# Attention output made feature by token: values as weights in two column strips, inverse sums widened by small products

## The reference, cut to what matters

```python
# per layer; concat over three groups of heads: A (recurrence, 256 columns), B and C (attention, 384 each)
o_a, s_a = hgrn_mixer(...)                       # (T, 256)
o_g = blocked_attention(q, k, v)                 # B: 6 query heads, 2 key/value heads, head width 64
o_w = banded_attention(q, k, v, k_ctx, v_ctx, sink)   # C: |t-s| <= 128, plus a sink logit in the sum
#   p = softmax(scores);  o = einsum('bkgqs,bskd->bqkgd', p, v)
x = x + g1 * (jnp.concatenate([o_a, o_g, o_w], axis=-1) @ w_out)
```

## Time and profile before

| | |
|---|---|
| median of 3 runs | 1646.12 us (1644.6 to 1650.44) |
| the profiled execution | 1649.72 us, span of the core 1647.9 us |
| TensorE matmul, busy | 1400.3 us, 85% |
| TensorE weight load, busy | 881.6 us, 53% |
| VectorE, busy | 566.8 us, 34% |
| ScalarE, busy | 358.0 us, 22% |
| GpSimd, busy | 210.7 us, 13% |

### The profile page before, as it was taken

How to read it: one execution, slowest core, us unless ns; L and a number is a source line. 1 busy time by engine, 2 the same in 40 slices (tenths; PEclk the granted TensorE clock), 3 DMA queues, 4 the chain that set the end, 5 groups by cost and what they waited for, 6 DMA issues and landing times. The chain is left out here.

```text
span 1647.9 us, 18619 instructions
## 1 busy us (share of the span) xinstructions
PE 1400.3 (85%) x6686; PEld 881.6 (53%) x6687; DVE 566.8 (34%) x1232; ACT 358.0 (22%) x777; POOL 210.7 (13%) x195
## 2 busy tenths in 40 slices
PE   3999988888899959999569999788888992999990
PEld 1577645676755534444245774566677552444440
DVE  0204623554523321111251163445454334111216
ACT  3210012333412201111151000233343110111112
POOL 0001204320000000000210002242101000000003
PEclk9999985999979869999769999689997995999995
DMA  9600023327052559999441000442301223699945
GB/s 343 218 0 4 4 102 106 107 99 297 2 206 95 195 199 332 368 363 377 173 178 27 4 1 4 154 147 91 125 4 36 100 102 115 223 369 369 368 161 204
DMA packets 114441, 262.64 MB, mean 159 GB/s; under 512 B 10152, under 2 KB 18880, under 8 KB 114368
## 3 DMA queue, kind: packets, MB, share of 16 engines
q1 hardware_dynamic: 100688, 211.84, 36.2%
q0 software_dynamic: 8064, 29.36, 4.7%
q10 hardware_dynamic: 5616, 20.45, 3.1%
HBM read 230.38 MB, written 34.41 MB: 161 GB/s over the span
## 5 line engine op out<-in xcount | busy, mean ns | idle before, releaser
L1801 PE MATMUL PS<-W,T 128*128 128x512 f32 x544 | 244.4, 603 | 4.5 <-ACT T L1854 4.5
L1801 PEld LDWEIGHTS PS<-W,T 128*128 128x128 f32 x544 | 104.9, 194 | 137.0 <-issue 131.3
L1474 PE MATMUL PS<-W,T 128*128 128x512 f32 x320 | 142.1, 598 | 0.0
L663 PE MATMUL PS<-W,hT 128*128 128x384 f32 x320 | 129.8, 487 | 0.0
L1819 PE MATMUL PS<-W,T 128*128 128x512 f32 x272 | 125.9, 607 | 1.4 <-ACT T L1878 1.4
L1020 PE MATMUL PS<-T 128*128 128x64 f32 x864 | 117.6, 292 | 3.2 <-DVE T L1237 3.2
L1020 PEld LDWEIGHTS PS<-T 128*128 128x128 f32 x864 | 110.7, 207 | 15.2 <-issue 8.3
L630 PE MATMUL PS<-hT,W 128*128 128x512 f32 x192 | 100.3, 605 | 0.0
L1919 DVE TENSOR_TENSOR T<-PS,T 128x256 f32<-128x256 f32 x34 | 14.5, 426 | 242.5 <-ACT T L1865 242.5
L1474 PEld LDWEIGHTS PS<-W,T 128*128 128x128 f32 x320 | 60.2, 193 | 69.0 <-issue 69.0
L994 PE MATMUL PS<-T 64*128 64x128 f32 (+2 forms) x480 | 67.2, 393 | 31.3 <-ACT T L1141 15.2
(11 more groups left out here) (270 smaller groups left out, 1898.5 us busy)
## 6 DMA issues: line engine op xcount, KB each, us to landing
W<-in_w_gate_up SPq DMA_DIRECT2D x34, 2048.0 KB, 12.1
W<-in_mod_w SPq DMA_DIRECT2D x19, 2048.0 KB, 8.1
W<-in_w_down SPq DMA_DIRECT2D x34, 1024.0 KB, 10.5
y_rows<-T ACTq DMA_DIRECT2D x34, 512.0 KB, 8.7
W<-in_w_in SPq DMA_DIRECT2D x8, 2048.0 KB, 14.8
W<-in_w_out SPq DMA_DIRECT2D x2, 4096.0 KB, 13.7
T<-gate_lines SPq DMA_DIRECT2D x16, 512.0 KB, 7.6
y_rows<-cst SPq DMA_DIRECT2D x1, 7680.0 KB, 27.7
```

What stands on the lines that cost most here:

```text
L663: pe.matmul(out[:, 0:QW].rearrange("p (j v d) -> p j v d", v=KVH, j=G), lhsT, w[:, 0:QW].rearrange("p (v j d) -> p j v d", v=KVH, j=G), st ...
L1474: last = pe.matmul(PS[:, 4 + b, :], oT[:, t % 2, k, :], wout[:, k, half(b)], start=(k == 0), stop=(k == KC - 1))
L1801: last = pe.matmul(PS[:, 2 + par, :], hgT[:, par, k, :], w[:, k, :], start=(k == 0), stop=(k == KC - 1))
```

## The change

The values become the stationary operand (128 keys x 64 features) and the turned weights the moving one (128 columns). The two key/value heads write to partitions 0 to 63 and 64 to 127 of one tile, each in one half of the columns of the array. The result is features by queries, so the inverse sum of a query is needed on all partitions: VectorE widens the four inverses of a group to 128x256 (`inverse`, in even steps), TensorE multiplies them with the identity (`spread_inverse`, in odd steps, four matmuls), ScalarE copies the 128x256 result (`copy_inverse`), and `outputs` multiplies by it. The attention part of `oall` then needs no turning; `turn_o` turns two blocks instead of eight, and `project` begins with the other six. The rows of the output weights are loaded in the new order, in five transfers, and the first expert's transfers start at other places, since `project` reads `oall` longer.

```diff
-                    sp.dma_start(wout[:, :, :], w_out[layer]...).then_inc(s_wo, 16)
+                    sp.dma_start(wout[:, 0:2, :], w_out[layer, 0:AW, :]...).then_inc(s_wo, 16)
+                    for w in range(2):
+                        for kv in range(KVH):
+                            first = AW + (KVH * w + kv) * G * HD
+                            sp.dma_start(wout[64 * kv:64 * kv + 64, 2 + G * w:2 + G * w + G, :],
+                                         w_out[layer, first:first + G * HD, :].rearrange("(j d) n -> d j n", d=HD))\
+                              .then_inc(s_wo, 16)
...
                     def turn(u):
                         pe.wait_ge(s_ax, u + 1)
+                        if u >= 2 and u % 2 == 0:
+                            pe.wait_ge(s_icols, u // 2)
...
+                    def spread_inverse(g):
+                        pe.wait_ge(s_inv, g + 1)
+                        pe.wait_ge(s_ax, min(2 * g + 3, U))
+                        for w in range(2):
+                            for kv in range(KVH):
+                                last = pe.matmul(PS[64 * kv:64 * kv + 64, 2, col(2 + w)], inv_wide[:, KVH * w + kv, :],
+                                                 ident, start=True, stop=True, skip_group_check=True)
+                        last.then_inc(s_ispread, 1)
...
-                        for kv in range(KVH):
-                            at = (KVH * wnd + kv) * HD
-                            for n, kt in enumerate(keys):
-                                last = pe.matmul(PS[:, 5, at:at + HD], src[:, col(kv * len(keys) + n)],
-                                                 v[:, kt, kv * HD:(kv + 1) * HD],
-                                                 start=(n == 0), stop=(n == len(keys) - 1))
+                        for n, kt in enumerate(keys):
+                            for kv in range(KVH):
+                                last = pe.matmul(PS[64 * kv:64 * kv + 64, 5, col(wnd)], v[:, kt, kv * HD:(kv + 1) * HD],
+                                                 src[:, col(kv * len(keys) + n)],
+                                                 start=(n == 0), stop=(n == len(keys) - 1), skip_group_check=True)
...
                         if step < U:
                             scores(step)
+                        if step >= 3 and step % 2:
+                            spread_inverse((step - 3) // 2)
                         sides(step, 0)
...
+                    def copy_inverse(g):
+                        act.wait_ge(s_ispread, g + 1)
+                        if g >= 1:
+                            act.wait_ge(s_aev, g)
+                        act.activation(inv_cols, PS[:, 2, 2 * P:4 * P], ACT.Copy).then_inc(s_icols, 1)
...
                     for step in range(U + 2):
+                        if step >= 3 and step % 2:
+                            copy_inverse((step - 3) // 2)
                         if step < U:
                             exponential(step)
...
+                    def inverse(g):
+                        den = rsum[:, g * GU:(g + 1) * GU]
+                        inv = rinv[:, g * GU:(g + 1) * GU]
+                        dve.wait_ge(s_esx, g + 1)
+                        link(dve.tensor_tensor(den[:, KVH:], den[:, KVH:], esx[:, g % 2, :], ALU.add))
+                        link(dve.reciprocal(inv, den))
+                        if g >= 1:
+                            dve.wait_ge(s_ispread, g)
+                        dve.tensor_copy(inv_wide, inv.unsqueeze(2).to_broadcast([P, GU, HD])).then_inc(s_inv, 1)
...
                     def outputs(g):
                         dve.wait_ge(s_apv, 2 * (g + 1))
-                        dve.wait_ge(s_esx, g + 1)
-                        link(dve.tensor_tensor(den[:, KVH:], den[:, KVH:], esx[:, g % 2, :], ALU.add))
-                        link(dve.reciprocal(inv, den))
-                        dve.tensor_tensor(oall[:, t, AW:D]...[:, j], PS[:, 5, 0:GU * HD]...,
-                                          inv.unsqueeze(2).to_broadcast([P, GU, HD]), ALU.mult)\
+                        dve.wait_ge(s_icols, g + 1)
+                        dve.tensor_tensor(oall[:, t, AW:D].rearrange("p (w j n) -> p j w n", w=2, j=G)[:, j],
+                                          PS[:, 5, 0:2 * P].rearrange("p (w n) -> p w n", w=2),
+                                          inv_cols.rearrange("p (w n) -> p w n", w=2), ALU.mult)\
...
                         if step < U:
                             maximum(step)
+                        if step >= 2 and step % 2 == 0:
+                            inverse((step - 2) // 2)
                         sides(step, 0)
...
-                    sp.wait_ge(s_ot, NT)
+                    sp.wait_ge(s_y, 2 * 3)
                     load_gate_up_of(sp, 0, 0)
-                    load_down_of(sp, 0, 0)
                     store_rows(3)
                     if layer + 1 < DEPTH:
                         for n in range(2, MOD1):
                             load_next_mod(sp, n)
+                    sp.wait_ge(s_y, 2 * NT)
+                    load_down_of(sp, 0, 0)
                     store_rows(4)
...
                     def turn_o(t):
-                        if t >= 1:
-                            pe.wait_ge(s_ote, t)
-                        for k in range(KC):
-                            last = pe.transpose(PS[:, k // 4, col(k % 4)], oall[:, t, col(k)], ident)
+                        if t >= 2:
+                            pe.wait_ge(s_ote, t - 1)
+                        for k in range(2):
+                            last = pe.transpose(PS[:, t % 2, col(k)], oall[:, t, col(k)], ident)
...
                     def project(t, b):
-                        pe.wait_ge(s_ote, t + 1)
                         if t >= 1:
                             pe.wait_ge(s_yp, 2 * t - 1 + b)
-                        for k in range(KC):
+                        for k in range(2, KC):
+                            pe.matmul(PS[:, 4 + b, :], oall[:, t, col(k)], wout[:, k, half(b)], start=(k == 2), stop=False)
+                        pe.wait_ge(s_ote, t + 1)
+                        for k in range(2):
```

## The result

The median went from 1648.28 us (1644.6 to 1653.58, 4 runs) to 1629.3 (1624.82 to 1636.59, 4 runs): a ratio of 0.9893, interval 0.9856 to 0.9931.

The account below looks back on a forecast made before the run. Attention has two nearly equal paths, `weigh` hardly ever on the longer; TensorE bounds the projection. Even +4.0, odd +3.1, step 4 -0.3, tail -2.5, projection -5.15: -0.85 a layer, -1.7 in both, 1644.4 us from the median; range 1633 to 1659.

Parts of the forecast that it names:

- the tail: Steps 30 and 31, without scores, at half clock: shorter weighing saves, less the last spread: -2.5 us a layer (0 to -3.5).
- the cold start of the projection: Projection's first product comes 3.9 us earlier but on the cold clock, for which 0.7 (0 to 1.8) is given back.
- rival B: Tail and projection start: 128-column strips bring the 2.4 GHz clock early; 9 us in two layers, 1635 us; chance 0.18.
- rival E: Attention loop: TensorE idles longer in even steps and its clock falls; three more spells, 13.5 us, 1658 us; chance 0.14.
- Projection without the clock: Projection, less turning: first product 3.9 us earlier, later turning 1.95 less; with 0.7 given back for the clock, -5.15 a layer.
- The edits costed at nothing: Five output-weight loads, moved expert loads, waits of the spread and for ScalarE's copy of the inverses: taken to cost 0.
- Strips side by side: `weigh`: records in two column strips overlap, 65 ns each instead of 109; twenty take 1.3 us instead of 2.2.
- Rival D: All odd steps: strips take turns, `weigh` saves nothing and spreads cost; some +9 us a layer, 1664 us; chance 0.11.
- Even steps: Attention loop: `inverse` (0.8 us) delays VectorE's level copy, 0.45 to 0.8 in each of seven steps; +4.0 us a layer.
- Odd steps: Attention loop: `spread_inverse` adds 0.8 us, partly hidden by waits or the shorter `weigh`; +3.1 us a layer (+1 to +5).
- steps 3 and 5: Early odd steps at half clock with little to weigh: only a 0.55 us wait hides the spread; +0.9 each.
- the 236 that was to mean "wrong": Attention stage under 236 us would show even steps not held by VectorE or a better clock; 241 to 245 meant right.

Follow-up runs that it names:

- e4: Kernel before plus unused 512-column products in steps 27 to 30 and after the projection's first turning; no strips, old projection: 1636.89 us, ratio 0.9911.
- e8: Kernel before, with each weighing record in steps 28 to 31 streaming its 64 value columns twice, 128 in all: 1642.88 us, ratio 0.9949.
- e5: Changed kernel with the old projection put back, all eight blocks turned and copied; strips and inverse sums stay: 1637.54 us, ratio 0.9926.
- e6: Kernel before plus two unused 128x256 products (about 0.8 us) ahead of the first level product of step 11 alone: 1642.86 us, ratio 0.9957.
- e3: Changed kernel plus two unused products of 256 and 128 columns behind most level products in steps 0 to 5: 1629.87 us, ratio 0.9891.

## Why the prediction was wrong, step by step

**The step that failed: the tail and the cold start of the projection.** The prediction took the new tail at the half clock that the earlier trace rows show for the old one and let the projection begin on it; rival B, in which the clock rises early, had 0.18. The tail was forecast at -2.5 us a layer and gave -5.7; the projection at -5.15 and gave -7.15. Together that is 10.4 us in two layers. e4 and e8 show the cause, a clock that stays up once the last steps stream more, without any other part of the change. The prediction's own argument held the answer: it had the records streaming twice the columns, in rival B and against rival E. It let the waits of steps 30 and 31 speak against that and gave B too little. B's time, 1635, is still 6 us too high, because the steps before the tail were mis-sized too: a second error of the same size, below.

**Projection without the clock: right.** 3.9 earlier and 1.95 of turning make 5.85 with the first part at half clock; at full clock e5 measures 4.6, of which 2.64 are the start and 1.98 the later turning. The edits costed at nothing stayed so: TensorE has one wait in the projection, 0.79 us at its start, and none for the output weights; no wait of the spread or of the turning for ScalarE's copy shows in the attention stage; and from the projection to the next attention 470.35 us became 469.99.

**Strips side by side: right.** 65 ns were taken for a record; 20 take 1.31 us. Rival D falls (its own terms add up to 9.85 a layer, not 9). The rule that it came from (the Trainium skill, page "TensorE: Matmul & The Clock Gate", Part 3, where weight loads overlap running matmuls only for another row group) is not borne out: all these records use the same 128 rows, and yet 20 take 1.31 us when the strips alternate and 2.02 head by head. Whether neighbours in one strip are slower for their weight loads or because they add to the same place in PSUM, no run separates.

**Even steps: right in mechanism, wrong in size.** The inverse took 0.63, not 0.8, and the steps lost 0.10 (10), 0.27 (12, 16), 0.28 (20) and 0.60 (24) instead of 0.45 to 0.8. With an inverse of 0.63 the prediction's own slack, 0.35 to nothing, gives these sizes in steps 12, 16, 20 and 24. Step 8 lost 2.87 instead (2.49 in layer 1), in a collision that the prediction did not look for. That steps 8 to 26 came to 4.1 and 3.7 in the two layers, near the +4.0 of the sum, is therefore luck.

**Odd steps: wrong.** Forecast +3.1 (which counts steps 13 and 21 at 0.1 each, though the text also has them among those that don't change). Spread and shorter weighing took 0.66 and 0.88 us in step 9, the 1.53 of the old weighing, and steps 9, 13, 15, 17, 19, 21, 23 and 25 of layer 0 changed by 0.01 or less, 27 by 0.20. Step 11 gave 3.24, and e6 shows why: the spread's delay moves GpSimd's start. In layer 1 steps 11, 13 and 15 were 9.97, 7.74 and 7.84, for 10.51, 6.53 and 6.54 before, at a granted clock of 0.68, 0.78 and 0.78 (1.00 in layer 0). That is rival E in small: such stretches stand in the loop of both kernels (before, steps 11 and 17 at 0.84 and 0.85). The odd steps 9 to 27 gave -3.1 in layer 0 and -1.0 in layer 1.

**Steps 0 to 7: not to be read from one execution.** They took 63.5 to 69.5 us in the eight layers of four profiles with the old attention, mean 67.8, and 63.2 to 72.6 in the ten layers of five with the new one (e3 apart), mean 68.3. The +0.9 forecast for each of steps 3 and 5 is not to be told from that.

In sum: the forecast was -1.7, the profiles show -19.5. Tail and projection account for -10.4 of the difference, the steps for -9.9 (+13.6 forecast, +3.7 measured), other stretches for +2.4. Of the signs that the prediction named, the 1.31 us, the wait of 1.33 in step 10 and the shorter projection came as said. The attention stage took 230.6 us in layer 0, under the 236 that was to mean "wrong", and 241.4 in layer 1, inside the 241 to 245: VectorE does hold the even steps, and the difference is step 11, the tail and the clock.

## What to carry to other kernels

Where a stage stands at half clock in the trace, ask first whether the change alters how much TensorE streams there; then the clock is the first term of the sum, not a rival. Look in each step at what GpSimd runs beside VectorE's small instructions: here shifts of 0.6 to 0.8 us gained or cost 3, half of it as a wait and half as low clock behind the wait. And put a new instruction behind the copy that the next engine waits for: the inverse in the other order was worth 6.2 us a layer in the loop, the strips 1.7.

## What the runs showed of the hardware

Some VectorE instructions stretch until the GpSimd product beside them ends: small ones with two operands in SBUF from 0.16 to 0.73 and 1.22 us (step 11 before) and 1.15 (e6), the 128x256 copy within SBUF from 0.29 to 1.09 (step 8 after). Others beside the same products do not: the maximum from PSUM kept its 1.49 and the reciprocal its 0.18, and an addition of two operands that began at 300.03, just as one product gave way to the next, its 0.15 (all in step 8 after). The Trainium skill, page "SBUF — State Buffer", section "SBUF: two separate sides", states such a rule: VectorE and GpSimd share one pair of ports, which an instruction of VectorE with two SBUF inputs, or in a mode that uses both port pairs, and one of GpSimd hold in turn, each for a whole instruction. The ends at 324.00 (step 11 before) and 324.71 (e6), where GpSimd's products end at 323.99 and 324.70, agree; in step 8 the copy ends 0.15 behind them. Read beside the old step 8, where GpSimd's products already ran under the place of the new copy (301.63 to 304.24, the level copy from 302.89), the rule would have pointed at it before the run.

At full clock a record of 128 columns took hardly longer than one of 64: 2.50 us against 2.44 for 20 (e8). And an extra stretch of work can shorten a kernel twice over, by the clock (e4, e8) or by moving a collision (e6).
